# Attention head of a two-layer decoder trunk: the order of ScalarE's and VectorE's work, and which engine copies the transposed probabilities

## The chip, the cores and the metric

One core of one Trainium2 chip runs the whole program. The metric is the time of one execution on the device in microseconds (us). The time before is 2576.37 us, the median of 3 runs (2575.84 to 2578.2).

## The reference, cut to what matters

A trunk of two equal layers over 512 tokens of width 1024, all in float32. Each layer adds a SwiGLU block, a token mixer and a second SwiGLU block to the residual stream. The change lies in the mixer:

```
rq, rk, rv, rg, sq, sk, sv, gate_r, gate_s = split(h @ w_in)
ret = head_groupnorm(retention(rope(rq), rope(rk), rv))       # 4 heads, dk 128, dv 256
ret = silu(rg) * ret
scores = sq_block . k_two_blocks * 64**-0.5, banded mask      # 16 query heads of 64, 2 key heads
m = max(scores, sink);  p = exp(scores - m)
probs = p / (sum(p) + exp(sink - m))
out = probs @ v_two_blocks
merged = sigmoid(gate_r) * (ret @ w_branch_ret) + sigmoid(gate_s) * (out @ w_branch_swa)
x = x + g2 * (merged @ w_out)
```

## The kernel before

**Units.** Every projection is cut into units of 128 output columns (`unit`, L1500). A unit is 8 steps of three products (L1486 to L1488): weights and activations are each split into a high and a low part, and high x high, high x low and low x high are summed in one PSUM bank, `pA[0]` or `pA[1]`, alternately. A unit's weights are loaded by SyncE's queue (`load`, L367) into `raw[s]`, ScalarE writes their high part (`split_weights`, L538), VectorE the low part (`split_weights`, L881), and TensorE starts the unit when the low part is there (`lo_ready`) and the bank is free (`bank_free`). The load of the next weights into the same `raw[s]` waits for that low part too.

**One head of the attention stage.** The stage has 4 turns a layer, 8 in all; here a turn is called a head, the first one head 0. A turn works on one retention head and on four steps of windowed attention, numbered h0 to h0+3, each with 2 query heads and 2 blocks of 128 queries. Between the small products of the attention steps TensorE computes six units: RQ and RK (retention query and key), G0 and G1 (retention gate), and SQ0 and SQ1 (the next turn's attention queries). TensorE's own order isn't changed: scores h0, unit RQ, (`variance` of the turn before), scores h0+1, unit RK, transposes h0, scores h0+2, unit G0, values h0, transposes h0+1, scores h0+3, unit G1, values h0+1, transposes h0+2, retention scores, unit SQ0, values h0+2, transposes h0+3, unit SQ1, values h0+3, retention values and the last retention scores.

**One step.** `swa_scores` (L1588) writes 1024 columns into banks 0 and 1 of `pM`. `maxima` (VectorE, L1150) adds the mask and moves them to `probs[w]` (L1154; its end, `masked`, lets TensorE write the next scores), and takes the row maxima. `exps` (ScalarE, L690) does four exponentials of 256 columns. `normalise` (VectorE, L1168) multiplies by the reciprocal sums. `swa_transposes` (L1597) makes eight 128x128 transposes into banks 2 and 3 of `pM`. `probs_out` copies them to `probs_t`: ScalarE bank 2 (L699 to L701), VectorE bank 3 (L1180 to L1182). `swa_values` (L1604) waits for both copies, and for one bank each:

```
pe.wait_ge(pt_act, no + 1)
pe.wait_ge(pt_dve, no + 1)
```

There is one `probs_t`, and two `probs[w]`, used in turn.

**Other work in the turn.** For the retention query and key ScalarE swaps the halves (`swap`, L680) and VectorE applies the rotation (`rope`, L1135, called by `retention_rope`, L1304). For the gate units ScalarE does Tanh (L799) and VectorE the product (`retention_gate`, L1308). `swa_out` (L703, L1184) splits the attention output of two steps into high and low part. `decay` (L1331) multiplies the retention scores by the decay and releases TensorE's `ret_values` (L1689, L1694). `start_query` swaps and rotates the next turn's queries.

**What sets the order.** Each engine has one queue in an order written out by hand: `middle` (ScalarE L781, VectorE L1300, TensorE L1659), then `tail` (L804, L1328, L1679), in a loop over three turns and once more written out for the last turn, which has no next query and no unit SQ1. An instruction that waits for a semaphore holds up all that is behind it on its engine.

Of the kernel before, what the change touches and what calls it, by code (L numbers as in the profile page):

```python
# [25 lines left out]
RH, DV = 4, 256  # L26
# [83 lines left out]
def decoder(nc, x, c, positions, norm_ffn1, norm_mix, norm_ffn2, final_norm, w_ada, b_ada,  # L110
# [5 lines left out]
    with ctx:  # L116
# [3 lines left out]
        def sem(name):  # L120
            return ctx.enter_context(nc.semaphore(name))
# [104 lines left out]
        swapped, rope_done = sem("swapped"), sem("rope_done")  # L226
        key_in, head_in = sem("key_in"), sem("head_in")
        scores, masked, max_ready, exp_ready, p_ready = sem("scores"), sem("masked"), sem("max_ready"), sem("exp_ready"), sem("p_ready")
        pt_ps, pt_act, pt_dve, o_ps, o_hi, o_done = (sem(n) for n in ("pt_ps", "pt_act", "pt_dve", "o_ps", "o_hi", "o_done"))
        st_ps, st_done, y_ps, ysq, ysum, y_free, var_ps = (sem(n) for n in ("st_ps", "st_done", "y_ps", "ysq", "ysum", "y_free", "var_ps"))  # L230
        mg_ready, mg_hi, mg_lo = sem("mg_ready"), sem("mg_hi"), sem("mg_lo")
        z_ready, y_first, y_last, o_first, o_last, stored = (sem(n) for n in ("z_ready", "y_first", "y_last", "o_first", "o_last", "stored"))
# [300 lines left out]
        def _(act):  # L533
# [163 lines left out]
                last.then_inc(exp_ready, 1)  # L697

            def probs_out(no):  # L699
                act.wait_ge(pt_ps, 2 * no + 1)  # L700
                act.activation(probs_t[:, 0:T], pM[:, 2, :], ACT.Copy).then_inc(pt_act, 1)  # L701

            def swa_out(no, tile):  # L703
                act.wait_ge(o_ps, no + 1)
# [21 lines left out]
            with act.Fori(0, DEPTH) as l:  # L726
# [54 lines left out]
                def middle(i):  # L781
                    b, g = pair_no(l, HEAD0) + 3 * i, gated_no(l, HEAD0) + 3 * i
                    rope0 = LAYER_ROPES * l + 1 + 4 * i
                    h0 = 4 * (RH * l + i)
                    exps(h0, 0)
                    swap(b + 1, 0, g + 1, rope0 + 2, pA[0], P // 2)
                    split_weights(b + 2, 0, UP_UNIT)
                    probs_out(h0)
                    exps(h0 + 1, 1)
                    swap(b + 1, 1, g + 1, rope0 + 3, pA[1], P // 2)  # L790
                    split_weights(b + 2, 1, UP_UNIT)
                    probs_out(h0 + 1)
                    exps(h0 + 2, 0)
                    for s in range(2):
                        act.wait_ge(unit_done, 2 * (b + 2) + s + 3)
                        act.wait_ge(rope_done, rope0 + 4 + 1)
                        if s:
                            act.wait_ge(bank_free[0], g + 2 + 2)
                        act.activation(side, pA[s][:, :], ACT.Tanh, scale=0.5).then_inc(swapped, 1)  # L799
                        split_weights(b + 3, s, UP_UNIT)  # L800
                        if s == 0:
                            exps(h0 + 3, 1)

                def tail(i, start):  # L804
                    h0 = 4 * (RH * l + i)
                    swa_out(2 * (RH * l + i), 2 * i)
                    probs_out(h0 + 2)
                    start(0)
                    probs_out(h0 + 3)
                    start(1)  # L810
                    swa_out(2 * (RH * l + i) + 1, 2 * i + 1)
                    act.wait_ge(y_ps, RH * l + i + 2)
                    for e in range(2):
                        act.activation(probs[1][:, T * e:T * (e + 1)], pM[:, 2 + e, :], ACT.Square).then_inc(ysq, 1)
# [48 lines left out]
        def _(dve):  # L863
# [313 lines left out]
                    last = dve.tensor_scalar(p, p, rden[w][:, n:n + 1], None, ALU.mult)  # L1177
                last.then_inc(p_ready, 1)

            def probs_out(no):  # L1180
                dve.wait_ge(pt_ps, 2 * no + 2)
                dve.tensor_copy(probs_t[:, T:2 * T], pM[:, 3, :]).then_inc(pt_dve, 1)  # L1182

            def swa_out(no, tile):  # L1184
                dve.wait_ge(o_hi, no + 1)
                dve.tensor_tensor(Alo[:, KT + tile, :], pO[:, :], Ahi[:, KT + tile, :].bitcast(F), ALU.subtract).then_inc(o_done, 1)
# [34 lines left out]
            with st.loop(0, DEPTH, LAYER_STEPS) as l:  # L1221
# [78 lines left out]
                def middle(i):  # L1300
                    b, side0, rope0, n0 = numbers(i)
                    h0 = 4 * n0

                    def retention_rope(n, tile):  # L1304
                        rope(rope0 + 2 + n, side0 + 2 + n, pA[n], cos_r, sin_r, [(tile, 0, P)], n)
                        split_weights(b + 2, n, UP_UNIT)

                    def retention_gate(n):  # L1308

                        dve.wait_ge(swapped, side0 + 4 + n + 1)  # L1310
                        dve.scalar_tensor_tensor(silu_g[:, n, :], side, 1.0, pA[n][:, :], ALU.add, ALU.mult).then_inc(bank_free[n], 1)
                        split_weights(b + 3, n, UP_UNIT)

                    retention_rope(0, rq)
                    normalise(h0, 0)
                    maxima(h0 + 1, l, i, 0, 1, 1)
                    probs_out(h0)
                    normalise(h0 + 1, 1)
                    retention_rope(1, rk)
                    maxima(h0 + 2, l, i, 1, 0, 0)  # L1320
                    probs_out(h0 + 1)
                    normalise(h0 + 2, 0)
                    retention_gate(0)
                    maxima(h0 + 3, l, i, 1, 1, 1)
                    retention_gate(1)
                    normalise(h0 + 3, 1)

                def tail(i, next_head):  # L1328
                    b, side0, rope0, n0 = numbers(i)
                    h0 = 4 * n0  # L1330

                    def decay(part):

                        dve.wait_ge(st_ps, RET_PARTS * n0 + part + 1)
                        for n in RET_BLOCKS[part]:
                            w, (bank, at) = T - P * n, RET_AT[n]
                            last = dve.tensor_tensor(ret_s[bank][:, at:at + w], pM[:, bank, at:at + w], K[:, bass.ds(K_DECAY + T * i, w)], ALU.mult)
                        last.then_inc(st_done, 1)

                    swa_out(2 * n0, 2 * i)  # L1340
                    probs_out(h0 + 2)
                    decay(0)
                    decay(1)
                    if next_head:
                        start_query(i + 1, 0)
                        split_weights(b + 4, 0, UP_UNIT)
                    probs_out(h0 + 3)
                    if next_head:
                        start_query(i + 1, 1)
                    swa_out(2 * n0 + 1, 2 * i + 1)  # L1350
                    decay(2)
                    if next_head:
                        split_weights(b + 4, 1, UP_UNIT)
                    for e in range(2):
                        dve.wait_ge(ysq, 2 * n0 + e + 1)
                        dve.tensor_tensor(XV[:, 2 * i + e, :], pM[:, 2 + e, :], silu_g[:, e, :], ALU.mult).then_inc(y_free, 1)
# [70 lines left out]
        def _(pe):  # L1427
# [169 lines left out]
            def swa_transposes(no, w):  # L1597
                pe.wait_ge(p_ready, no + 1)
                for a in range(2):
                    for n in range(4):  # L1600
                        last = pe.transpose(pM[:, 2 + a, P * n:P * (n + 1)], probs[w][:, T * a + P * n:T * a + P * (n + 1)], ident)
                    last.then_inc(pt_ps, 1)

            def swa_values(no, half):  # L1604
                pe.wait_ge(pt_act, no + 1)
                pe.wait_ge(pt_dve, no + 1)
                for n in range(2):
                    blk = 2 * half + n
                    for kt in range(0 if blk else 1, 2):
# [192 lines left out]
```

## Time and profile before

| What | us |
|---|---|
| median of 3 runs | 2576.37 |
| the profiled execution's own time | 2574.76 |
| its span, first to last instruction | 2572.9 |
| attention stage of layer 0 | 508.50 to 732.60 |
| attention stage of layer 1 | 1748 to 1975 |
| one turn in the loop (scores h0 to the next scores h0, 564.47 to 620.53) | 56.06 |

The profile is one execution. Times in its timeline count from the start of the span. A timeline row says start, duration, engine, line, operation, what it writes and reads, and how many instructions are merged in it; a bracket says how long the engine had been idle and which instruction released it. TensorE's products overlap: one of 512 columns lasts 0.39 us, but the next starts 0.23 us after it. TensorE is PE in the rows, VectorE DVE, ScalarE ACT, GpSimd POOL, and PEld is TensorE's loading of weights.

### The profile page before, as it was taken

What the parts mean: (1) busy time and instruction counts of PE and PEld (TensorE: products, weight loads), DVE (VectorE), ACT (ScalarE), POOL (GpSimd) and SP (SyncE); (2) the same over time, 40 slices, a digit from 0 to 9 for tenths busy, and PEclk for the clock granted to TensorE, in tenths of its full rate; (3) what the DMA queues carried; (4) which work ended last, traced back from release to release, by engine and by line L of the source; (5) the groups of instructions that cost most, each with busy time, mean ns of one, the idle gap of its engine ahead of it and who ended that gap; (6) DMA issues with size and microseconds to landing.
All of it is one profiled execution on the core that took longest, in us unless ns stands there. A gap on an engine that the chain in (4) does not pass through costs nothing.

```text
span 2572.9 us, 35974 instructions
## 1 busy us (share of the span) xinstructions
PE 2492.2 (97%) x11573; PEld 2039.4 (79%) x11573; DVE 1535.1 (60%) x2341; ACT 874.2 (34%) x1324; POOL 213.1 (8%) x167
## 2 busy tenths in 40 slices
PE   5999999999999999999999999999999999999998
PEld 4788888877778878888878888887777888788887
DVE  6876778677743367633467767777665445633333
ACT  2321233545423243223332222345543333321232
POOL 5100003000000040000040000120000001200001
PEclk7899999999999999999999999999999999999999
DMA  6465664321223425533326656632111343233332
GB/s 221 123 201 174 182 198 127 123 62 53 57 74 98 128 85 170 158 88 98 103 86 196 186 173 195 180 115 74 57 57 50 98 131 98 82 104 92 90 110 78
DMA packets 494472, 307.19 MB, mean 119 GB/s; under 512 B 8936, under 2 KB 488504, under 8 KB 493752
## 3 DMA queue, kind: packets, MB, share of 16 engines
q1 hardware_dynamic: 426808, 239.10, 31.5%
q10 hardware_dynamic: 67584, 67.12, 8.2%
q8 instruction: 39, 0.64, 0.1%
q14 instruction: 41, 0.34, 0.0%
HBM read 299.89 MB, written 6.29 MB: 119 GB/s over the span
## 4 chain that ended last, share of the span: by engine, by line
PE 77%; DVE 12%; ACT 5%; issue 4%; POOL 1%; DVEq 0%; DMA 0%; ACTq 0%; SPq 0%; POOLq 0%
PE ps_proj L1486 24%; PE ps_proj L1488 24%; PE ps_proj L1487 23%; ACT sb_scratch L695 2%; DVE sb_w_lo L886 2%; DVE sb_small L1157 1%; DVE sb_scratch L1154 1%; PE ps_mid L1642 1%; PE ps_mid L1643 1%; PE ps_mid L1644 1%; DVE sb_scratch L1177 1%; POOL sb_scratch L470 1%; ACT sb_w_hi L542 1%; DVE sb_h_lo L953 1%; DVE sb_scratch L898 1%
## 5 line engine op out<-in xcount | busy, mean ns | idle before, releaser
L1486 PE MATMUL ps_proj<-sb_a_hi,sb_w_hi 128*128 128x512 f32 x1888 | 736.5, 390 | 3.0 <-DVE sb_w_lo L886 3.0
L1488 PE MATMUL ps_proj<-sb_a_hi,sb_w_lo 128*128 128x512 f32 x1888 | 734.8, 389 | 0.0
L1487 PE MATMUL ps_proj<-sb_a_lo,sb_w_hi 128*128 128x512 f32 x1888 | 734.7, 389 | 0.0
L542 ACT ACTIVATE sb_w_hi<-sb_raw 128x1024 fp32r<-128x1024 f32 (+1 forms) x388 | 431.0, 1111 | 872.0 <-PE ps_proj L1488 832.5
L886 DVE TENSOR_TENSOR sb_w_lo<-sb_raw,sb_w_hi 128x1024 fp32r<-128x1024 f32 (+1 forms) x388 | 503.5, 1298 | 310.5 <-ACT sb_w_hi L542 295.1
L1486 PE MATMUL ps_proj<-sb_h_hi,sb_w_hi 128*128 128x512 f32 x1280 | 509.9, 398 | 10.8 <-DVE sb_w_lo L886 6.3
L1487 PE MATMUL ps_proj<-sb_h_lo,sb_w_hi 128*128 128x512 f32 x1280 | 502.4, 392 | 0.0
L1488 PE MATMUL ps_proj<-sb_h_hi,sb_w_lo 128*128 128x512 f32 x1280 | 501.8, 392 | 0.0
L1486 PEld LDWEIGHTS ps_proj<-sb_a_hi,sb_w_hi 128*128 128x128 f32 x1888 | 354.4, 188 | 78.9 <-issue 2.9
L1488 PEld LDWEIGHTS ps_proj<-sb_a_hi,sb_w_lo 128*128 128x128 f32 x1888 | 354.4, 188 | 73.9
L1487 PEld LDWEIGHTS ps_proj<-sb_a_lo,sb_w_hi 128*128 128x128 f32 x1888 | 354.4, 188 | 73.2
L1486 PEld LDWEIGHTS ps_proj<-sb_h_hi,sb_w_hi 128*128 128x128 f32 x1280 | 242.5, 189 | 72.0 <-issue 20.3
L1488 PEld LDWEIGHTS ps_proj<-sb_h_hi,sb_w_lo 128*128 128x128 f32 x1280 | 242.6, 190 | 51.9
L1487 PEld LDWEIGHTS ps_proj<-sb_h_lo,sb_w_hi 128*128 128x128 f32 x1280 | 242.8, 190 | 48.6
L898 DVE SCALAR_TENSOR_TENSOR sb_scratch<-sb_scratch,sb_c_act 128x256 f32<-128x256 f32 x448 | 220.4, 492 | 16.1
L455 POOL TENSOR_TENSOR sb_scratch<-sb_scratch 128x512 f32<-128x512 f32 x42 | 69.0, 1644 | 1755.7 <-ACT sb_scratch L553 1754.9
L1041 DVE SCALAR_TENSOR_TENSOR sb_x_or_values<-ps_proj,sb_half_gate,sb_x_or_values 128x512 f32 (+1 forms) x80 | 60.0, 750 | 204.4 <-PE ps_proj L1488 202.7
L1064 DVE TENSOR_TENSOR sb_scratch<-sb_scratch,ps_proj 128x512 f32<-128x512 f32 x80 | 55.0, 687 | 179.2 <-PE ps_proj L1488 179.2
L640 ACT ACTIVATE sb_scratch<-ps_proj 128x512 f32<-128x512 f32 x80 | 47.9, 599 | 300.5 <-PE ps_proj L1488 300.5
L953 DVE SCALAR_TENSOR_TENSOR sb_h_lo<-sb_x_or_values,sb_gain,sb_h_hi 128x512 fp32r<-128x512 f32 (+1 forms) x48 | 71.2, 1492 | 8.4 <-ACT sb_h_hi L575 7.9
L695 ACT ACTIVATE sb_scratch<-sb_scratch,sb_small 128x256 f32<-128x256 f32 x128 | 63.1, 494 | 0.0
L1067 DVE TENSOR_TENSOR sb_a_lo<-sb_scratch,sb_a_hi 128x512 f32 (+1 forms) x80 | 54.7, 684 | 0.0
(171 smaller groups left out, 1804.9 us busy)
## 6 DMA issues: line engine op xcount, KB each, us to landing
sb_raw<-in_ffn_w_up SPq DMA_DIRECT2D x176, 512.0 KB, 3.8
sb_scratch<-in_w_ada ACTq DMA_DIRECT2D x128, 512.0 KB, 4.2
sb_raw<-in_w_in SPq DMA_DIRECT2D x100, 512.0 KB, 3.8
sb_raw<-in_ffn_w_down SPq DMA_DIRECT2D x64, 704.0 KB, 4.5
sb_raw<-in_w_branch_swa SPq DMA_DIRECT2D x16, 512.0 KB, 3.5
sb_raw<-in_w_branch_ret SPq DMA_DIRECT2D x16, 512.0 KB, 3.6
sb_raw<-in_w_out SPq DMA_DIRECT2D x16, 512.0 KB, 3.5
sb_scratch<-in_w_ada SPq DMA_DIRECT2D x14, 512.0 KB, 7.9
```

The costliest lines, as they stand in the source:

```text
L455: pool.tensor_tensor(square_sum, square_sum, squares[:, k % 2, :], ALU.add).then_inc(sq_used, 1)
L542: act.activation(Whi[s][:, 0:n], raw[s][:, 0:n], ACT.Copy).then_inc(hi_ready, 1)
L695: last = act.activation(p, p, ACT.Exp, bias=neg_m[w][:, n:n + 1], scale=HD ** -0.5, accum_out=row_sum[w][:, n:n + 1])
L886: dve.tensor_tensor(Wlo[s][:, 0:n], raw[s][:, 0:n], Whi[s][:, 0:n].bitcast(F), ALU.subtract).then_inc(lo_ready, 1)
L898: ins = dve.scalar_tensor_tensor(ada_acc, ada_raw[s][:, k % 4, :], col, ada_acc, ALU.mult, ALU.add)
L953: dve.scalar_tensor_tensor(Hlo[:, k, :], XV[:, k, :], gain[:, bass.ds(k, 1)], Hhi[:, k, :].bitcast(F), ALU.mult, ALU.subtract).then_inc(gx ...
L1041: dve.scalar_tensor_tensor(XV[:, m, :], pA[s][:, :], half_gate[:, bass.ds(m, 1)], XV[:, m, :], ALU.mult, ALU.add).then_inc(bank_free[s], 1)
L1064: dve.tensor_tensor(work, side, pA[1][:, :], ALU.mult).then_inc(bank_free[1], 1)
L1067: dve.tensor_tensor(Alo[:, i, :], work, Ahi[:, i, :].bitcast(F), ALU.subtract).then_inc(act_lo, 1)
L1486: pe.matmul(bank, Whi[s][:, w], hi, start=first, stop=False)
L1487: pe.matmul(bank, Whi[s][:, w], lo, start=False, stop=False)
L1488: return pe.matmul(bank, Wlo[s][:, w], hi, start=False, stop=last)
```

## The change

The copy of the transposed probabilities is one ScalarE instruction of 1024 columns. It is released once all eight transposes are done, where before each bank had a release of its own. VectorE's copy and the semaphore `pt_dve` are gone. On ScalarE the swap of unit RK comes ahead of the copy of step h0; the Tanh of G0 ahead of the copy of step h0+1; the Tanh of G1, `swa_out` and the copy of step h0+2 ahead of the exponentials of step h0+3. On VectorE `normalise` of h0 comes ahead of the first rotation, the second rotation ahead of `normalise` of h0+1, the product of G0 ahead of `normalise` of h0+2; the low part of G0's weights stays behind the first rotation, those of G1, SQ0 and SQ1 come behind `normalise` of h0+1, h0+2 and h0+3; `swa_out` comes ahead of the product of G1, and the first two parts of `decay` ahead of `normalise` of h0+3.

```diff
 # ScalarE
             def probs_out(no):
-                act.wait_ge(pt_ps, 2 * no + 1)
-                act.activation(probs_t[:, 0:T], pM[:, 2, :], ACT.Copy).then_inc(pt_act, 1)
+                act.wait_ge(pt_ps, no + 1)
+                act.activation(probs_t.rearrange("p (a t) -> p a t", a=2), pM[:, 2:4, :], ACT.Copy).then_inc(pt_act, 1)
...
                     exps(h0, 0)
                     swap(b + 1, 0, g + 1, rope0 + 2, pA[0], P // 2)
                     split_weights(b + 2, 0, UP_UNIT)
+                    swap(b + 1, 1, g + 1, rope0 + 3, pA[1], P // 2)
                     probs_out(h0)
                     exps(h0 + 1, 1)
-                    swap(b + 1, 1, g + 1, rope0 + 3, pA[1], P // 2)
                     split_weights(b + 2, 1, UP_UNIT)
-                    probs_out(h0 + 1)
-                    exps(h0 + 2, 0)
-                    for s in range(2):
+
+                    def gate(s):
                         act.wait_ge(unit_done, 2 * (b + 2) + s + 3)
                         act.wait_ge(rope_done, rope0 + 4 + 1)
                         if s:
                             act.wait_ge(bank_free[0], g + 2 + 2)
                         act.activation(side, pA[s][:, :], ACT.Tanh, scale=0.5).then_inc(swapped, 1)
-                        split_weights(b + 3, s, UP_UNIT)
-                        if s == 0:
-                            exps(h0 + 3, 1)
+
+                    gate(0)
+                    probs_out(h0 + 1)
+                    exps(h0 + 2, 0)
+                    split_weights(b + 3, 0, UP_UNIT)
+                    gate(1)
+                    swa_out(2 * (RH * l + i), 2 * i)
+                    probs_out(h0 + 2)
+                    exps(h0 + 3, 1)
+                    split_weights(b + 3, 1, UP_UNIT)
 
                 def tail(i, start):
                     h0 = 4 * (RH * l + i)
-                    swa_out(2 * (RH * l + i), 2 * i)
-                    probs_out(h0 + 2)
                     start(0)
                     probs_out(h0 + 3)
                     start(1)
 # VectorE
-            def probs_out(no):
-                dve.wait_ge(pt_ps, 2 * no + 2)
-                dve.tensor_copy(probs_t[:, T:2 * T], pM[:, 3, :]).then_inc(pt_dve, 1)
...
                     def retention_rope(n, tile):
                         rope(rope0 + 2 + n, side0 + 2 + n, pA[n], cos_r, sin_r, [(tile, 0, P)], n)
-                        split_weights(b + 2, n, UP_UNIT)
...
                         dve.scalar_tensor_tensor(silu_g[:, n, :], side, 1.0, pA[n][:, :], ALU.add, ALU.mult).then_inc(bank_free[n], 1)
-                        split_weights(b + 3, n, UP_UNIT)
...
+                    normalise(h0, 0)
                     retention_rope(0, rq)
-                    normalise(h0, 0)
+                    split_weights(b + 2, 0, UP_UNIT)
                     maxima(h0 + 1, l, i, 0, 1, 1)
-                    probs_out(h0)
+                    retention_rope(1, rk)
                     normalise(h0 + 1, 1)
-                    retention_rope(1, rk)
+                    split_weights(b + 2, 1, UP_UNIT)
                     maxima(h0 + 2, l, i, 1, 0, 0)
-                    probs_out(h0 + 1)
+                    retention_gate(0)
                     normalise(h0 + 2, 0)
-                    retention_gate(0)
+                    split_weights(b + 3, 0, UP_UNIT)
                     maxima(h0 + 3, l, i, 1, 1, 1)
+                    swa_out(2 * n0, 2 * i)
                     retention_gate(1)
+                    decay(i, 0)
+                    decay(i, 1)
                     normalise(h0 + 3, 1)
+                    split_weights(b + 3, 1, UP_UNIT)
...
                 def tail(i, next_head):
...
-                    swa_out(2 * n0, 2 * i)
-                    probs_out(h0 + 2)
-                    decay(0)
-                    decay(1)
                     if next_head:
                         start_query(i + 1, 0)
                         split_weights(b + 4, 0, UP_UNIT)
-                    probs_out(h0 + 3)
                     if next_head:
                         start_query(i + 1, 1)
                     swa_out(2 * n0 + 1, 2 * i + 1)
-                    decay(2)
+                    decay(i, 2)
 # TensorE
                 for a in range(2):
                     for n in range(4):
                         last = pe.transpose(pM[:, 2 + a, P * n:P * (n + 1)], probs[w][:, T * a + P * n:T * a + P * (n + 1)], ident)
-                    last.then_inc(pt_ps, 1)
+                last.then_inc(pt_ps, 1)
...
                 pe.wait_ge(pt_act, no + 1)
-                pe.wait_ge(pt_dve, no + 1)
```

## Rows read from the trace of the kernel before

**Rows 1.** The page, part 1: busy time of each engine over the span.

```profile
PE 2492.2 (97%) x11573; PEld 2039.4 (79%) x11573; DVE 1535.1 (60%) x2341; ACT 874.2 (34%) x1324; POOL 213.1 (8%) x167
```

**Rows 2.** Busy time by window, layer 0's attention stage: stretch, length, engines, clock, DMA.

```profile
508.50:732.60 224.10, 212.59 (x1178) 162.80 (x1177) 155.13 (x286) 111.04 (x256) 10.06 (x11) 1.00 0.20 57
```

**Rows 3.** TensorE's waits, 508 to 735 us: total us, times, longest.

```profile
PE ps_o L1612 <- DVE sb_scratch L1182: 7.5, 5, 1.7
PE ps_mid L1593 <- DVE sb_scratch L1154: 2.3, 4, 1.1
PE ps_mid L1694 <- DVE sb_scratch L1337: 1.7, 3, 0.6
```

**Rows 4.** Timeline of TensorE, head 1 of layer 0.

```profile
578.63 1.03 PE L1601 MATMUL ps_mid<-sb_consts,sb_scratch 128*128 128x128 f32 x8
579.59 1.14 PE L1593 MATMUL ps_mid<-sb_scratch 64*128 64x256 f32 x8
...
586.04 0.39 PE L1488 MATMUL ps_proj<-sb_h_hi,sb_w_lo 128*128 128x512 f32 x1
586.36 0.88 PE L1612 MATMUL ps_o<-sb_scratch 128*64 128x128 f32 x12
587.17 1.09 PE L1601 MATMUL ps_mid<-sb_consts,sb_scratch 128*128 128x128 f32 x8
588.68 1.14 PE L1593 MATMUL ps_mid<-sb_scratch 64*128 64x256 f32 x8 [0.42 <-DVE sb_scratch L1154]
...
597.37 1.89 PE L1686 MATMUL ps_mid<-sb_scratch 128*128 128x512 f32 x6
...
604.36 0.39 PE L1488 MATMUL ps_proj<-sb_h_hi,sb_w_lo 128*128 128x512 f32 x1
606.42 0.88 PE L1612 MATMUL ps_o<-sb_scratch 128*64 128x128 f32 x12 [1.67 <-DVE sb_scratch L1182]
...
619.47 1.13 PE L1694 MATMUL ps_mid<-sb_scratch 128*128 128x256 f32 x4 [0.57 <-DVE sb_scratch L1337]
```

**Rows 5.** Timeline of TensorE in head 0 and in head 3, the last.

```profile
532.62 1.14 PE L1593 MATMUL ps_mid<-sb_scratch 64*128 64x256 f32 x8 [1.10 <-DVE sb_scratch L1154]
...
719.26 1.09 PE L1601 MATMUL ps_mid<-sb_consts,sb_scratch 128*128 128x128 f32 x8
721.23 1.09 PE L1612 MATMUL ps_o<-sb_scratch 128*64 128x128 f32 x16 [0.88 <-DVE sb_scratch L1182]
```

**Rows 6.** Timeline of VectorE, head 1.

```profile
582.88 0.16 DVE L1171 TENSOR_TENSOR sb_small<-sb_small 128x4 f32<-128x4 f32 x1 [1.59 <-ACT sb_scratch L695]
...
584.35 0.69 DVE L1139 TENSOR_TENSOR sb_scratch<-ps_proj,sb_cos_r 128x512 f32<-128x512 f32 x1
...
586.28 1.22 DVE L886 TENSOR_TENSOR sb_w_lo<-sb_raw,sb_w_hi 128x1024 fp32r<-128x1024 f32 x1
587.41 1.22 DVE L1154 TENSOR_TENSOR sb_scratch<-ps_mid,sb_consts 128x1024 f32<-128x1024 f32 x1
...
590.36 0.69 DVE L1182 COPY sb_scratch<-ps_mid 128x512 f32<-128x512 f32 x1
...
605.59 0.68 DVE L1182 COPY sb_scratch<-ps_mid 128x512 f32<-128x512 f32 x1
```

**Rows 7.** Timeline of ScalarE, head 1.

```profile
580.67 0.21 ACT L692 ACTIVATE sb_small<-sb_small 128x4 f32<-128x4 f32 x1 [0.81 <-DVE sb_small L1166]
...
582.87 0.60 ACT L686 ACTIVATE sb_scratch<-ps_proj 64x512 f32<-64x512 f32 x1
...
584.10 1.06 ACT L542 ACTIVATE sb_w_hi<-sb_raw 128x1024 fp32r<-128x1024 f32 x1
...
592.52 0.58 ACT L799 ACTIVATE sb_scratch<-ps_proj 128x512 f32<-128x512 f32 x1
...
602.73 0.58 ACT L701 ACTIVATE sb_scratch<-ps_mid 128x512 f32<-128x512 f32 x1
```

**Rows 8.** The page, part 6: SyncE's loads of the mixer's weights, us to landing.

```profile
sb_raw<-in_w_in SPq DMA_DIRECT2D x100, 512.0 KB, 3.8
```

More of the change, by code:

```diff
@@ L228, in decoder @@
         scores, masked, max_ready, exp_ready, p_ready = sem("scores"), sem("masked"), sem("max_ready"), sem("exp_ready"), sem("p_ready")
-        pt_ps, pt_act, pt_dve, o_ps, o_hi, o_done = (sem(n) for n in ("pt_ps", "pt_act", "pt_dve", "o_ps", "o_hi", "o_done"))
+        pt_ps, pt_act, o_ps, o_hi, o_done = (sem(n) for n in ("pt_ps", "pt_act", "o_ps", "o_hi", "o_done"))
         st_ps, st_done, y_ps, ysq, ysum, y_free, var_ps = (sem(n) for n in ("st_ps", "st_done", "y_ps", "ysq", "ysum", "y_free", "var_ps"))
@@ L1311, in retention_gate, with decay @@
                         dve.scalar_tensor_tensor(silu_g[:, n, :], side, 1.0, pA[n][:, :], ALU.add, ALU.mult).then_inc(bank_free[n], 1)
-                        split_weights(b + 3, n, UP_UNIT)
+                    normalise(h0, 0)
                     retention_rope(0, rq)
-                    normalise(h0, 0)
+                    split_weights(b + 2, 0, UP_UNIT)
                     maxima(h0 + 1, l, i, 0, 1, 1)
-                    probs_out(h0)
+                    retention_rope(1, rk)
                     normalise(h0 + 1, 1)
-                    retention_rope(1, rk)
+                    split_weights(b + 2, 1, UP_UNIT)
                     maxima(h0 + 2, l, i, 1, 0, 0)
-                    probs_out(h0 + 1)
+                    retention_gate(0)
                     normalise(h0 + 2, 0)
-                    retention_gate(0)
+                    split_weights(b + 3, 0, UP_UNIT)
                     maxima(h0 + 3, l, i, 1, 1, 1)
+                    swa_out(2 * n0, 2 * i)
                     retention_gate(1)
+                    decay(i, 0)
+                    decay(i, 1)
                     normalise(h0 + 3, 1)
+                    split_weights(b + 3, 1, UP_UNIT)
+                def decay(i, part):
+                    dve.wait_ge(st_ps, RET_PARTS * numbers(i)[3] + part + 1)
+                    for n in RET_BLOCKS[part]:
+                        w, (bank, at) = T - P * n, RET_AT[n]
+                        last = dve.tensor_tensor(ret_s[bank][:, at:at + w], pM[:, bank, at:at + w], K[:, bass.ds(K_DECAY + T * i, w)], ALU.mult)
+                    last.then_inc(st_done, 1)
                 def tail(i, next_head):
@@ L1330, in tail @@
                     h0 = 4 * n0
[L1332 to L1338, printed above, removed]
-                    swa_out(2 * n0, 2 * i)
-                    probs_out(h0 + 2)
-                    decay(0)
-                    decay(1)
                     if next_head:
```

## The prediction

> **What bounds the kernel now.** I read the page's busy times first [rows 1]: TensorE is busy for 97% of the span, VectorE for 60%, ScalarE for 34%. A change in the order of ScalarE and VectorE can therefore only win what TensorE waits. The busy time by window [rows 2] shows how much that is where the change lies: in layer 0's attention stage TensorE works 212.59 of 224.10 us, so some 11.5 us are open there, at a granted clock of 1.00 (the 2.4 GHz level), which these short waits haven't lowered. VectorE works 155 us of the stage and ScalarE 111, so neither is full. The list of waits [rows 3] names the 11.5 us: 7.5 us of the value products (L1612) for VectorE's copy L1182, 2.3 us of the scores (L1593) for VectorE's masking L1154, and 1.7 us of the last retention values (L1694) for the decay L1337. Layer 1's stage has the same three lines with the same totals.
>
> TensorE's timeline of head 1 [rows 4] shows where in the turn. Scores h0+3 start at 588.68 after 0.42 us idle. Values h0+2, behind unit SQ0, start at 606.42 after 1.67 us idle. The last retention values wait 0.57 us at 619.47. Head 0 has 1.10 us at the first place, and head 3 has an additional wait of 0.88 us at values h0+3, which there stand right behind their transposes [rows 5].
>
> The waits cost a little more than the idle figures, which start from modelled ends. Between transposes and scores nothing waits at 578.63 and 579.59, 0.96 us apart; at 587.17 and 588.68 they are 1.51 apart, so that wait costs 0.55. From a unit's last product to values it is 0.32 us without a wait (586.04 to 586.36) and 2.06 with it (604.36 to 606.42): 1.74 [rows 4].
>
> **The change part by part, walked through head 1.** Up to the transposes at 578.63 nothing moves. `normalise` of h0 fits into VectorE's idle time ahead of the first rotation, and the low part of G0's weights and the maxima of h0+1 end no later than before.
>
> *Scores h0+3.* They need the masking of h0+2. Before, VectorE did `normalise`, the rotation of RK, the low part of G1 and only then the masking, from 587.41 to 588.63 [rows 6]; the rotation lay in the chain behind the exponentials. Now it lies beside them. The new chain: unit RK ends at about 578.8, ScalarE begins its swap at 579.0, which takes 1.23 (582.87 to 584.10) [rows 7], to 580.2. Then the copy of 1024 columns. The trace has no such copy from PSUM. Its lower bound is ScalarE's 1024 columns from SBUF, 1.06; its upper bound two copies of 512 at 0.58 to 0.60, so 1.20 [rows 7]. I take 1.06, the nearest in shape: 581.3. Exponentials 2.20 (580.67 to 582.87): 583.5. `normalise` 1.47 (582.88 to 584.35): 585.0. Low part of G1 1.13 (586.28 to 587.41): 586.1. Masking 1.22: 587.3 [rows 6]. The rotation of RK, 1.93 (584.35 to 586.28), runs from 580.2 to 582.1 while ScalarE does copy and exponentials. TensorE could start the scores at 587.17 + 0.96 = 588.13. So the wait goes, with 0.8 us to spare, 0.6 with the dearer copy. Head 0 stands the same way to its chain: its 1.10 us goes too.
>
> *Retention scores.* These need the masking of h0+3. The chain begins at G0's end, 586.4. Tanh to 587.2; copy of h0+1 behind the transposes' end (587.17 + 1.09) to 589.4, by when the maxima of h0+2 are there as well (586.1 + 2.95, the 2.95 from 587.41 to 590.36 [rows 6]); exponentials to 591.6; `normalise` to 593.0; low part of SQ0 to 594.2; masking to 595.4. TensorE is there at 597.37 - 0.55 = 596.8 [rows 4]: 1.4 us to spare. What waits behind ScalarE's Tanh here is exactly this copy and these exponentials, so this is the chain that could go wrong.
>
> *Values h0+2.* Before, VectorE's copy stood behind the product of G1, a low part, `normalise` and `swa_out`, and began at 605.59 [rows 6], although ScalarE's half had begun at 602.73 [rows 7]. Now ScalarE's copy follows the transposes at 597.0 and ends at 598.1, and VectorE's `swa_out` ends at 597.8. TensorE is there at 604.36 + 0.32 - 0.55 = 604.1. The 1.74 us goes, with 6 to spare. What is late next: `normalise` of h0+3 (exponentials 598.1 to 600.3, the two decays by then done, 601.8) against the transposes at 604.9, and the low part of SQ1 at 602.9 against its unit at 605.9; 3 us each. Later waits up to the end of the turn have 2.5 us or more by the same working.
>
> *Last retention values.* Swap, rotation, `swa_out` and decay stand in the same order behind unit SQ1, so the 0.57 us stays.
>
> *Values h0+3 in head 3.* Here nothing covers the copy: the transposes end at 720.35, and the values start 0.88 later, at 721.23 [rows 5], with VectorE's copy of 0.69 [rows 6] in between. Now it is 1.06 (to 1.20) on ScalarE: 0.4 us more, 0.5 at most.
>
> *What costs nothing, and what hides it.* VectorE loses 32 copies of 0.69, 22 us; it is not the bound. ScalarE goes from 32 x 0.59 to 32 x 1.06, 15 us more, hidden by units of 24 products, 5.5 us each; without them each copy would cost the 0.4 of head 3. SyncE's loads wait for the low parts, which come at 586.1, 594.2 and 602.9 against 587.4, 595.9 and 603.5; they are issued sooner, and a load lands in 3.8 us [rows 8], long before its split. No DMA is issued from the moved steps, GpSimd's waits hang on TensorE alone. One wait fewer before 32 groups of values is worth nothing, or at best 0.1 us a group, 3 us in all, since values show a gap of 0.32 where products show 0.23; I take nothing and keep the 3 us for the lower end.
>
> **Sum.** Of the idle figures of a layer 2.3 + (7.5 - 0.88) = 8.9 go [rows 3, 5]. The four waits of either kind cost 0.13 and 0.07 more than shown: + 0.8. The last copy: - 0.4. That is 9.3 a layer, 18.7 in both with roundings. The profiled execution's own time is 2574.76 (span 2572.9), which gives 2556.1; it lies 1.6 below the median of the runs, which gives 2557.7, my forecast, 0.73% less.
>
> **A rule that speaks against it.** The values of a step are released when the later copy ends. Half the copy takes VectorE 0.69, and ScalarE 0.58 beside it, and one engine needs 1.06 at least for the whole [rows 6, 7]. The Trainium skill, "PSUM — Partial Sum Buffer", Specifications (TRN2), says that ScalarE and VectorE can read PSUM in parallel at full bandwidth if they don't meet in a bank; by that rule the split copy is the better one, and taking it away costs time. The trace agrees only where TensorE has nothing in between.
>
> **The rivals.**
> *The copy lies on the path everywhere.* Each of the 32 groups of values would start some 0.37 us later instead of 2: 30 x 0.37 = 11 us back, 2568.8. The parallel reading of two banks, above, is the reason one could give. Against it: in three of four steps a unit of 5.5 us lies between transposes and values.
> *The scores' wait stays.* The chain to the masking of h0+2 has only 0.8 us to spare, and now holds swap, copy and exponentials in one ScalarE queue. If the chain is 1.4 us longer than I have it, the 2.3 + 4 x 0.13 = 2.8 us a layer remain: 5.6 more, 2563.3.
> *ScalarE's queue becomes the bound, slower than before.* Place: Tanh of G0 ahead of the copy of h0+1 and the exponentials of h0+2, and through `normalise`, low part and masking the retention scores. It decides from 1.4 us on. To end 5 us above the time before it has to give back 18.7 + 5, or 3.0 us in each of 8 heads, so the chain must be 4.4 us longer than I have it. Priced at 4.6, TensorE waits 3.2 us a head, 25.6 in all: 2583. For it: the chain is serial over two engines. Against it: Tanh stood directly behind exponentials before too and took 0.58 us [rows 7], with no reload of the activation table before it.
> That the change doesn't do what it says can hardly be: the orders are written out by hand.
>
> **How the numbers follow.** The forecast has 0.80, the scores' wait that stays (wholly or in part) 0.10, the copy on the path 0.04, slower 0.03, other small losses that leave the time within 5 us of before 0.03. A measurement of this kernel can tell about 0.2%, 5 us, from no change. Faster: 0.94; within 0.2%: 0.03; slower: 0.03. The range reaches down by the 3 us for the fewer waits, with 0.7 for the runs' spread, to 2554.0, and up to the second rival, 2563.5.
>
> **What would show it.** TensorE's waits should name L1154 and the copy nowhere but in head 3, there with 1.2 to 1.3 us; L1694 keeps 3 waits of 0.57 a layer. A turn takes 53.8 us instead of 56.06. ScalarE's copy takes 1.06 to 1.20 us, 32 times. VectorE's L1154 of step h0+2 ends some 0.8 us before its scores. Scores still waiting for L1154 would be the second rival; a new line with L1177, L1154 before L1686, or an additional table load, the third. The prediction is wrong if the turn isn't between 53.3 and 54.6 us.

## The result, and the profile after

The kernel after takes 2557.01 us, the median of 4 runs (2555.9 to 2558.24), against 2576.11 us for the kernel before (4 runs, 2574.15 to 2578.2). The ratio is 0.9926, with a 95% interval of 0.9909 to 0.9943: faster by 0.74%. The forecast was 2557.7, with a range of 2554.0 to 2563.5. The profiled execution of after took 2558.24 us, its span is 2556.5.

The page, part 1, of the kernel after answers to [rows 1]:

```profile
PE 2493.7 (98%) x11573; PEld 2041.7 (80%) x11573; DVE 1515.6 (59%) x2309; ACT 887.8 (35%) x1324; POOL 212.8 (8%) x167
```

TensorE does the same 11573 products in nearly the same busy time (1.5 us more), but in a span that is 16.4 us shorter. VectorE has 32 instructions and 19.5 us less busy time, ScalarE as many instructions as before and 13.6 us more.

Busy time by window of layer 0's attention stage in the kernel after, the answer to [rows 2]:

```profile
508.20:723.20 215.00, 212.16 (x1178) 162.69 (x1178) 145.62 (x270) 117.86 (x256) 9.93 (x11) 1.00 0.21 59
```

The stage is 9.1 us shorter (224.10 to 215.00), TensorE's work in it is the same: 212.6 and 212.2 us. Some 2.8 us of it are open where it was 11.5.

TensorE's waits in that stage of the kernel after (total us, times, longest), the answer to [rows 3]:

```profile
PE ps_mid L1691 <- DVE sb_scratch L1336: 1.7, 3, 0.6
PE ps_o L1609 <- ACT sb_scratch L701: 1.1, 1, 1.1
```

The scores' wait for the masking is gone, and of the 7.5 us of the value products one wait of 1.1 us is left, the last turn's. The wait for the decay is as it was. Layer 1 has the same two lines with the same totals.

TensorE's timeline in head 1 of the kernel after, the answer to [rows 4]; its turn begins 3.2 us sooner than before:

```profile
575.45 1.03 PE L1599 MATMUL ps_mid<-sb_consts,sb_scratch 128*128 128x128 f32 x8
576.41 1.14 PE L1591 MATMUL ps_mid<-sb_scratch 64*128 64x256 f32 x8
...
583.99 1.09 PE L1599 MATMUL ps_mid<-sb_consts,sb_scratch 128*128 128x128 f32 x8
585.01 1.13 PE L1591 MATMUL ps_mid<-sb_scratch 64*128 64x256 f32 x8
...
593.74 1.89 PE L1683 MATMUL ps_mid<-sb_scratch 128*128 128x512 f32 x6
...
600.73 0.39 PE L1486 MATMUL ps_proj<-sb_h_hi,sb_w_lo 128*128 128x512 f32 x1
601.05 0.88 PE L1609 MATMUL ps_o<-sb_scratch 128*64 128x128 f32 x12
...
614.10 1.13 PE L1691 MATMUL ps_mid<-sb_scratch 128*128 128x256 f32 x4 [0.57 <-DVE sb_scratch L1336]
615.16 1.14 PE L1591 MATMUL ps_mid<-sb_scratch 64*128 64x256 f32 x8
```

Between the second transposes and the scores there are 1.02 us, between the last product of SQ0 and the values 0.32, and neither row has a bracket. The previous turn's scores h0 stand at 561.28, so a turn takes 53.88 us, against 56.06.

VectorE's timeline of the same head, and below it ScalarE's, the answers to [rows 6] and [rows 7]:

```profile
577.10 0.69 DVE L1143 TENSOR_TENSOR sb_scratch<-ps_proj,sb_cos_r 128x512 f32<-128x512 f32 x1 [1.03 <-ACT sb_scratch L687]
...
580.11 0.16 DVE L1175 TENSOR_TENSOR sb_small<-sb_small 128x4 f32<-128x4 f32 x1 [1.00 <-ACT sb_scratch L695]
...
581.58 1.22 DVE L890 TENSOR_TENSOR sb_w_lo<-sb_raw,sb_w_hi 128x1024 fp32r<-128x1024 f32 x1
582.72 1.22 DVE L1158 TENSOR_TENSOR sb_scratch<-ps_mid,sb_consts 128x1024 f32<-128x1024 f32 x1
...
590.84 1.22 DVE L1158 TENSOR_TENSOR sb_scratch<-ps_mid,sb_consts 128x1024 f32<-128x1024 f32 x1
...
593.83 0.69 DVE L1186 TENSOR_TENSOR sb_a_lo<-ps_o,sb_a_hi 128x512 f32 x1
```

```profile
575.78 0.59 ACT L686 ACTIVATE sb_scratch<-ps_proj 64x512 f32<-64x512 f32 x1 [4.95 <-PE ps_proj L1486]
...
577.00 1.02 ACT L701 ACTIVATE sb_scratch<-ps_mid 128x1024 f32<-128x1024 f32 x1
577.92 0.20 ACT L692 ACTIVATE sb_small<-sb_small 128x4 f32<-128x4 f32 x1
...
583.37 0.60 ACT L798 ACTIVATE sb_scratch<-ps_proj 128x512 f32<-128x512 f32 x1 [2.34 <-PE ps_proj L1486]
...
593.94 1.02 ACT L701 ACTIVATE sb_scratch<-ps_mid 128x1024 f32<-128x1024 f32 x1 [0.29 <-PE ps_mid L1599]
```

The rotation of unit RK (577.10) now runs while ScalarE copies (577.00) and takes the exponentials (577.92); `normalise` follows at 580.11. The masking of h0+2 (582.72) ends at 583.94, and scores h0+3, which wait for it, start at 585.01: 1.0 us to spare.

The last turn of the kernel after, the answer to [rows 5]: the last transposes, ScalarE's copy, and the values that wait for it.

```profile
709.60 1.09 PE L1599 MATMUL ps_mid<-sb_consts,sb_scratch 128*128 128x128 f32 x8
710.73 1.02 ACT L701 ACTIVATE sb_scratch<-ps_mid 128x1024 f32<-128x1024 f32 x1 [5.01 <-PE ps_mid L1599]
711.81 1.09 PE L1609 MATMUL ps_o<-sb_scratch 128*64 128x128 f32 x16 [1.11 <-ACT sb_scratch L701]
```

### The profile page after: what moved, and what is told of

Its sections match the earlier page's. It is cut to its first block, busy times and chain, and to the rows that moved or that the text cites. A ratio compares the mean times of both kernels' runs of the same rounds, so it can differ in the third digit from the quotient of the medians.

```text
span 2556.5 us, 35860 instructions
## 1 busy us (share of the span) xinstructions
PE 2493.7 (98%) x11573; PEld 2041.7 (80%) x11573; DVE 1515.6 (59%) x2309; ACT 887.8 (35%) x1324; POOL 212.8 (8%) x167
## 4 chain that ended last, share of the span: by engine, by line
PE 90%; DVE 5%; issue 2%; ACT 1%; POOL 1%; DMA 0%; DVEq 0%; SPq 0%; ACTq 0%; POOLq 0%
PE ps_proj L1484 27%; PE ps_proj L1486 27%; PE ps_proj L1485 27%; PE ps_mid L1591 1%; PE ps_mid L1599 1%; PE ps_mid L1639 1%; PE ps_mid L1641 1%; PE ps_mid L1640 1%; PE ps_o L1609 1%; POOL sb_scratch L470 1%; DVE sb_h_lo L957 1%; DVE sb_scratch L902 1%; PE ps_mid L1691 1%; PE ps_mid L1683 1%; DVE sb_scratch L1202 0%
## 5 line engine op out<-in xcount | busy, mean ns | idle before, releaser
L686 ACT ACTIVATE sb_scratch<-ps_proj 32x512 f32<-32x512 f32 (+1 forms) x48 | 28.3, 590 | 81.6 <-PE ps_proj L1486 81.3
```

## The experiments

Theory: the gain comes from two serial chains over ScalarE and VectorE, which the new order shortens; the copy's engine matters little. First rival: it comes from who copies. The runs were made in two groups, each on one chip beside the kernel before: e1, e2, e3 and e8 beside 12 runs of it with a median of 2576.13 us, e4 to e7 beside 15 runs with 2575.19. "Above after" and "below after" compare a median with the 2557.01 us of the section above, so with e4 to e7 they can be off by the 0.9 us between the groups. Times in head 1 are of layer 0.

Medians of this kernel move by a microsecond or two. The traces tell small differences better: the time from a layer's first scores to its last row of retention values agrees between the two layers within 0.1 us. Here it is for both layers together.

| Kernel | both stages, us | against before | against after |
|---|---|---|---|
| before | 431.9 | | |
| after | 413.8 | -18.1 | |
| e1_copy_alone | 426.9 | -5.0 | |
| e2_order_alone | 413.4 | -18.5 | -0.4 |
| e3_first_half_old | 417.1 | | +3.3 |
| e8_second_half_old | 416.0 | | +2.2 |
| e4_one_spare | 413.8 | | 0.0 |
| e5_four_spare | 425.7 | | +12.0 |
| e6_decay_first | 410.2 | | -3.6 |
| e7_both | 409.5 | | -4.3 |

**The copy alone, on the old order** (e1_copy_alone)

```diff
 # on the kernel before
-                act.wait_ge(pt_ps, 2 * no + 1)
-                act.activation(probs_t[:, 0:T], pM[:, 2, :], ACT.Copy).then_inc(pt_act, 1)
+                act.wait_ge(pt_ps, no + 1)
+                act.activation(probs_t.rearrange("p (a t) -> p a t", a=2), pM[:, 2:4, :], ACT.Copy).then_inc(pt_act, 1)
 # and VectorE's probs_out with its four calls, and pt_dve, are gone
```

> The kernel before, with the copy of all 1024 columns on ScalarE and none on VectorE, both orders as before. Theory (the gain comes from the order of the two queues): values h0+2 no longer wait for VectorE's copy, but the low part of swa_out right ahead of it on VectorE ended at 605.67, so they start some 0.65 us sooner a head and keep about 1.0 us of idle time; the wait at scores h0+3 stays (0.42 to 0.5), values h0+3 of the last head wait 0.4 longer. Together 8 x 0.65 - 2 x 0.4 = 4.4 us less than before, about 2571.7. Rival (the gain comes from who copies, that is from VectorE's 22 us): all of it is here, 2557 to 2559.

Measured: 2569.88 us (8 runs), ratio 0.9975 (0.9964 to 0.9985), 6.3 us below the 2576.13 of before. TensorE's waits in layer 0's attention stage:

```profile
PE ps_o L1603 <- DVE sb_a_lo L1182: 3.8, 4, 1.0
PE ps_mid L1585 <- DVE sb_scratch L1154: 2.3, 4, 1.1
PE ps_mid L1685 <- DVE sb_scratch L1331: 1.7, 3, 0.6
PE ps_o L1603 <- ACT sb_scratch L701: 1.1, 1, 1.1
```

Expected were 4.4 us less, and the stages became 5.0 shorter. So the copy's removal alone gives about a third of the gain, as its interval has it 4 to 9 us. The values then wait for the low part of `swa_out`, which had stood directly ahead of VectorE's copy: 0.95 us four times in place of 1.65. The scores' 2.3 us is untouched.

**The order alone, with the split copy** (e2_order_alone)

```diff
 # on the kernel after; both copies, releases and waits as in the kernel before, and VectorE's copies here:
+                    probs_out(h0)
                     retention_rope(1, rk)
...
                     retention_gate(0)
+                    probs_out(h0 + 1)
                     normalise(h0 + 2, 0)
...
                     decay(i, 1)
+                    probs_out(h0 + 2)
                     normalise(h0 + 3, 1)
...
                         split_weights(b + 4, 0, UP_UNIT)
+                    probs_out(h0 + 3)
```

> The kernel after, with the split copy put back (ScalarE bank 2, VectorE bank 3, a release for each bank), VectorE's copies ahead of the second rotation, ahead of normalise of h0+2, of normalise of h0+3, and behind the first next query. Theory: VectorE's 0.69 us fits into its idle time each time, so TensorE's waits are those of after, and the last head's is 0.4 us shorter: 0.7 to 0.9 us below after, about 2556.3, a turn of 53.9. Rival (who copies): most of the gain is lost, 2570 or more. The PSUM rule as a price everywhere would give 11 us below after, 2546.

Measured: 2557.82 us (5 runs, 2554.59 to 2558.93), ratio 0.9926 (0.9912 to 0.9939). TensorE's waits:

```profile
PE ps_mid L1700 <- DVE sb_scratch L1343: 1.7, 3, 0.6
PE ps_o L1618 <- DVE sb_scratch L1186: 0.9, 1, 0.9
```

The order alone gives the whole gain, as far as the runs can tell. The two parts don't add: the 6.3 us of the copy's removal are contained in the 18.3 of the order, since the copy only cost something where the order had it stand late. The last turn's wait is 0.9 instead of 1.1 us; the 0.4 us in two layers that this is worth show in the stages' time and can't be seen in the medians. The first rival falls.

**The first half of the turn in the old order** (e3_first_half_old)

```diff
 # on the kernel after
-                    swap(b + 1, 1, g + 1, rope0 + 3, pA[1], P // 2)
                     probs_out(h0)
                     exps(h0 + 1, 1)
+                    swap(b + 1, 1, g + 1, rope0 + 3, pA[1], P // 2)
...
-                    retention_rope(1, rk)
                     normalise(h0 + 1, 1)
+                    retention_rope(1, rk)
```

> The kernel after, with only the swap and the rotation of unit RK put back behind the exponentials and normalise of h0+1. Theory: the masking of h0+2 ends at about 585.4 in head 1 instead of 583.9, so scores h0+3 wait about 0.4 us again (1.1 in head 0), 5 to 6 us in all: 2562.5; values h0+2 don't wait. Rival (the second half of the turn is the only one that counts, the first has slack): no wait at the scores, 2557.

Measured: 2560.16 us (5 runs, 2559.76 to 2563.17), ratio 0.9939 (0.9926 to 0.9953), 3.2 us above after. In TensorE's waits one line has come back:

```profile
PE ps_mid L1591 <- DVE sb_scratch L1158: 1.4, 4, 0.4
```

So the rotation in the chain is what made the scores wait. From the transposes' start to the masking's end it is 9.94 us in head 1 (576.62 to 586.56), where after has 8.49 (575.45 to 583.94). The rotation adds 1.93, and the swap, which no longer stands ahead of the copy, gives some 0.5 back; of the 1.45 us, 1.1 were to spare, and 0.35 is the wait.

The wait is 0.35 us in head 0 too, where the kernel before had 1.10 and the theory expected 1.1 again. The start of head 0's exponentials of h0+1 shows the difference, first in the kernel before, then in this run:

```profile
524.58 0.20 ACT L692 ACTIVATE sb_small<-sb_small 128x4 f32<-128x4 f32 x1 [1.43 <-DVE sb_small L1166]
```

```profile
524.32 0.20 ACT L692 ACTIVATE sb_small<-sb_small 128x4 f32<-128x4 f32 x1
```

Before, ScalarE stood idle for 1.43 us, waiting for the maxima of h0+1, which VectorE took only behind `normalise` of h0 (1.46 us, 520.11 to 521.57). In e3 that `normalise` still stands ahead of the first rotation, and the exponentials follow the copy without a pause, 15.36 us from the head's first scores where it was 16.03: 0.67 of the 0.75 us between the two waits. So a second piece of the new order helps head 0. This is read from the rows; no run undid that piece alone.

**The second half in the old order** (e8_second_half_old)

```diff
 # on the kernel after, ScalarE
-                    gate(0)
                     probs_out(h0 + 1)
                     exps(h0 + 2, 0)
+                    gate(0)
                     split_weights(b + 3, 0, UP_UNIT)
+                    exps(h0 + 3, 1)
                     gate(1)
+                    split_weights(b + 3, 1, UP_UNIT)
                     swa_out(2 * (RH * l + i), 2 * i)
                     probs_out(h0 + 2)
-                    exps(h0 + 3, 1)
-                    split_weights(b + 3, 1, UP_UNIT)
 # VectorE
-                    retention_gate(0)
                     normalise(h0 + 2, 0)
+                    retention_gate(0)
                     split_weights(b + 3, 0, UP_UNIT)
                     maxima(h0 + 3, l, i, 1, 1, 1)
+                    retention_gate(1)
+                    split_weights(b + 3, 1, UP_UNIT)
+                    normalise(h0 + 3, 1)
                     swa_out(2 * n0, 2 * i)
-                    retention_gate(1)
                     decay(i, 0)
                     decay(i, 1)
-                    normalise(h0 + 3, 1)
-                    split_weights(b + 3, 1, UP_UNIT)
```

> The kernel after, with the second half of the turn (from the copy of h0+1 on) in the order of before on ScalarE and VectorE, but with the copy on ScalarE alone. Theory: scores h0+3 don't wait; VectorE's low part of swa_out comes behind the product of G1, a low part and normalise of h0+3 and ends at about 601.5 of head 1, where TensorE wants the values at 601.05: 0.4 to 0.5 us a head, 3.5 to 4 us in all, 2561. Rival (both halves are needed in full, as the wait at values h0+2 was 1.67): the wait is back at 1.2 or more a head, 2567 or more.

Measured: 2560.42 us (5 runs, 2558.97 to 2562.53), ratio 0.9938 (0.9924 to 0.9951), 3.4 us above after. In TensorE's waits the values wait again, for `swa_out`:

```profile
PE ps_o L1609 <- DVE sb_a_lo L1186: 0.8, 4, 0.2
```

The wait is 0.2 us a head, where 0.4 to 0.5 was expected, and nothing like the 1.67 of before. Its four waits a layer and what starts cost above the idle time explain the 2.2 us by which the stages are longer; the rest of the 3.4 is within the spread of the runs. With e3 and e8 over 80% of the gain stays (16.0 and 15.7 us below before, of 19.1): with the one copy and the other half of the new order each chain misses its time by little.

**How much the first chain has to spare** (e4_one_spare, e5_four_spare)

```diff
 # on the kernel after, ScalarE; 1 copy in the first run, 4 in the second, each behind the one before it
                     probs_out(h0)
+                    for n in range(4):
+                        if n:
+                            act.wait_ge(spared, 4 * (RH * l + i) + n)
+                        act.activation(spare[:, :], cos_r[:, :], ACT.Copy).then_inc(spared, 1)
                     exps(h0 + 1, 1)
```

> The kernel after, with one spare ScalarE copy of 512 columns into an unused tile between the copy of h0 and the exponentials of h0+1 (0.5 to 0.65 us more in that chain, 8 times). Theory: in the profile of after the masking of h0+2 ends at 583.94 and its scores start at 585.01, so the chain has some 1.0 us to spare: no wait at scores h0+3, time as after, 2557. Rival (the chain is at its limit, and every microsecond in ScalarE's queue costs): + 8 x 0.55 = 4.4 us, 2561.

> The same with four spare copies one behind the other, 2.4 to 2.6 us more in the chain. Theory: TensorE waits 1.4 to 1.6 us at scores h0+3 in each of 8 heads, 12 us in all, 2569; the later waits stay away, because what is late at the scores is late for TensorE too. Rival (slack of more than 2.5 us, as the later chains have): time as after.

Measured: 2558.19 us with one spare copy (4 runs, 2557.45 to 2559.25; ratio 0.9933, 0.9917 to 0.9948). This median, 1.2 us above after, lies between theory and rival and doesn't decide; the trace does, with the waits of after and stages as long as its own. With four it is 2570.09 us (10 runs, 2567.45 to 2571.81; ratio 0.9979, 0.997 to 0.9989), 13.1 above after, and the stages are 12.0 longer, where 12 was expected. ScalarE's timeline with four, then TensorE's waits:

```profile
579.98 2.62 ACT L795 ACTIVATE sb_spare<-sb_cos_r 128x512 f32<-128x512 f32 x4
582.51 0.19 ACT L694 ACTIVATE sb_small<-sb_small 128x4 f32<-128x4 f32 x1
```

```profile
PE ps_mid L1597 <- DVE sb_scratch L1164: 4.7, 4, 1.2
...
PE ps_mid L1605 <- DVE sb_scratch L1187: 0.8, 4, 0.2
```

The chain is 2.5 us longer (579.98 to 582.51), and 1.4 us a head appear as idle time, in two places: 1.17 at the scores, and 0.19 already at the transposes of h0+1, which wait for `normalise`. With the 1.0 us to spare the sum closes. The theory had missed the transposes: in after `normalise` of h0+1 ends 2.3 us ahead of them (581.67 against 583.99), less than the 2.5 us added.

**The wait that was left** (e6_decay_first)

```diff
 # on the kernel after, VectorE's tail
-                    swa_out(2 * n0 + 1, 2 * i + 1)
                     decay(i, 2)
+                    swa_out(2 * n0 + 1, 2 * i + 1)
```

> The kernel after, with the last part of decay ahead of the second swa_out on VectorE. Theory: in after decay starts at 613.63 behind a rotation that ends at 613.1 and swa_out of 0.6, while its scores are there at 611.8; it now starts at 613.03, ends 0.6 sooner, and the wait of 0.57 at the last retention values goes, three times a layer: 3.4 us, 2553.6. Rival (the wait moves to ScalarE's squares and the next maxima): the idle time at L1691 goes and the turn stays at 53.9.

Measured: 2553.78 us (5 runs, 2552.94 to 2557.75), ratio 0.9918 (0.9905 to 0.9932), 3.2 us below after by the medians (2.3 by the ratios to before) and 3.6 by the stages' time, where 3.4 was expected. One wait is left in the stage, and the turn, from 561.28 to the row below, takes 53.28 us:

```profile
PE ps_o L1609 <- ACT sb_scratch L701: 1.1, 1, 1.1
```

```profile
614.56 1.14 PE L1591 MATMUL ps_mid<-sb_scratch 64*128 64x256 f32 x8
```

So nothing behind the retention values took the wait's place.

**The split copy where nothing covers it** (e7_both)

```diff
 # on e6_decay_first, for the last turn's last step alone
+            def half_probs_out(no):       # ScalarE
+                act.wait_ge(pt_ps, no + 1)
+                act.activation(probs_t[:, 0:T], pM[:, 2, :], ACT.Copy).then_inc(pt_act, 1)
+            def half_probs_out(no):       # VectorE
+                dve.wait_ge(pt_ps, no + 1)
+                dve.tensor_copy(probs_t[:, T:2 * T], pM[:, 3, :]).then_inc(pt_dve, 1)
...
+                    if isinstance(i, int):
+                        pe.wait_ge(pt_dve, l + 1)
                     swa_values(h0 + 3, 1).then_inc(o_ps, 1)
```

> As e6, and in the last turn of a layer alone the last step's copy is split again, ScalarE bank 2 and VectorE bank 3, both released after all eight transposes. Theory: there the wait falls from 1.11 to about 0.8 (copies of 0.69 and 0.60 beside each other instead of 1.02), 0.6 us in both layers below e6, about 2553.0; a 4.0 us win on after.

Measured: 2554.52 us (5 runs, 2551.83 to 2555.92), ratio 0.9914 (0.9901 to 0.9928), 0.7 above e6 where 0.6 below it was expected. ScalarE's and VectorE's copies in the last turn, and TensorE's wait in the stage:

```profile
710.13 0.60 ACT L705 ACTIVATE sb_scratch<-ps_mid 128x512 f32<-128x512 f32 x1 [5.01 <-PE ps_mid L1609]
710.13 0.69 DVE L1190 COPY sb_scratch<-ps_mid 128x512 f32<-128x512 f32 x1 [3.25 <-PE ps_mid L1609]
```

```profile
PE ps_o L1619 <- DVE sb_scratch L1190: 0.8, 1, 0.8
```

The two copies start together and last as long as alone, and the wait falls by 0.3 us, as expected. The stages are 0.7 us shorter than in e6, which is below what the medians can tell; as the runs don't separate the two, the simpler e6 is the version to keep.

## Why the prediction was right

**Scores h0+3.** The forecast had the chain from RK's end to the masking's end at 8.5 us (578.8 to 587.3) with 0.8 to spare; the trace of after has 8.3 us and 1.0 to spare. The copy of 1024 columns, which the trace of before did not show, took 1.02 us (bounds 1.06 to 1.20, value taken 1.06, so it fell a little below the lower bound). The wait is gone in all heads, and e3 shows that it was the rotation's place; in head 0 the earlier `normalise` of h0 has a part in it, which the forecast had not worked out.

**Retention scores.** The masking of h0+3 was to end at 595.4 against scores due at 596.8. After, it takes VectorE 1.22 us from 590.84 and ends at 592.06, and the retention scores start at 593.74 without a wait: 1.7 us to spare, where 1.4 was forecast. No run lengthened this chain.

**Values h0+2.** The 1.74 us a head went; ScalarE's copy ends at 594.96 (593.94 + 1.02) and the values start at 601.05, so the forecast 6 us to spare are 6.1.

**Last retention values.** Predicted to stay at 0.57, and it is there at 614.10. e6 shows that it hung on the order of two VectorE instructions.

**Values h0+3 in the last turn.** Predicted 1.2 to 1.3 us, measured 1.11, so the difference to before is 0.23, not 0.4. The forecast took the copies' difference, 1.06 - 0.69. Measured it is 1.02 - 0.69 = 0.33, and the values start 0.06 us behind the copy's end (711.75 to 711.81), where it was 0.15 before:

```profile
720.39 0.69 DVE L1182 COPY sb_scratch<-ps_mid 128x512 f32<-128x512 f32 x1 [0.83 <-PE ps_mid L1601]
```

This copy ends at 721.08, and the values start at 721.23. Why they follow sooner now was not tried.

**One wait fewer before the values** was taken as nothing. The gap from the last product to the values is 0.32 us as before (600.73 to 601.05), so where the copy is long done it is nothing.

**The sum.** Predicted 9.3 us a layer; in both layers the stage became 9.1 shorter, 18.1 in all against 18.7. The idle figures went as forecast. What the waits cost beyond them was taken as 0.8 us a layer and comes to 0.4: at scores h0+3 the forecast took 0.96 us between transposes and scores without a wait, and in after it is 1.02, so that wait had cost 0.49 and not 0.55. The last copy's 0.23 in place of 0.4 makes up a part of it. The medians differ by 19.1, with an interval of 14.7 to 23.4, so that 18.7 and 19.1 lie so close together is in part luck. The two profiled executions differ by only 16.4 us in span; what the clock has to do with that is told below.

**What the prediction read wrongly, without harm.** A unit lies between transposes and values not in three of four steps but in all four of a turn, but for the last turn's last step: in 15 of 16 a layer. That speaks against the copy on the path more strongly than the prediction had it. Its list of waits leaves out the transposes of h0+1, which wait for `normalise` and had 2.3 us to spare, less than the later waits. And VectorE's 22 us are a sum of durations; its busy time, in which neighbouring instructions overlap, fell by 19.5.

**The rivals.** The copy on the path everywhere: no; values wait for the copy only in the last turn, and e2 with the split copy is not faster. In e7 the halves take 0.60 and 0.69 us beside each other, as long as alone in the kernel before, and that brings 0.3 us a layer. The Trainium skill's rule, that ScalarE and VectorE can read PSUM in parallel at full bandwidth if they don't meet in a bank ("PSUM — Partial Sum Buffer", Specifications (TRN2)), is borne out by this. The scores' wait that stays: the chain needed 1.0 us more to bring it back, and e4 and e5 stand on the two sides of that. ScalarE's queue as the bound: TensorE's L1683 doesn't wait for VectorE's L1158, there is no additional table load (9 in both kernels), and a turn takes 53.88 us.

## What to carry to other kernels

When an engine of 60% load holds up one of 97%, follow the serial chain from the event that starts it to the wait that ends last, and take out of it what could run beside it: here a rotation of 1.93 us moved into the time in which the other engine did its exponentials. Where work of TensorE covers it, a copy's cost is where it stands in a queue, not how long it lasts: to take 19.5 us off VectorE's busy time was worth 5 to 6 us in the old order and nothing that could be measured in the new one. Only in the last turn, where nothing covers it, does its length count. Before you move work to another engine, write down the slack of every wait behind it; of the waits that went away, the scores' has the least, 1.0 us, and four spare copies showed what comes beyond it, in part at transposes that the list had left out.

## What the runs showed of the hardware that was not expected

In both kernels the granted clock of TensorE falls for some microseconds at the start of each SwiGLU block but the first, where TensorE has worked with hardly a pause and then waits some 3 us for the reciprocal root (3.4, 2.7 and 3.4 us in the kernel before). At the same place of the mixer it waits 1.0 us, and the clock stays at 1.00. How far the mean falls differs between executions. Three stretches of 30 us from 10 us ahead of that place, in busy time by window (the clock is the third value from the end): the kernel before, then the kernel after.

```profile
945.00:975.00 30.00, 26.59 (x127) 22.28 (x126) 25.27 (x37) 12.51 (x18) 14.45 (x12) 0.94 0.20 56
1315.00:1345.00 30.00, 27.31 (x131) 23.14 (x130) 24.46 (x37) 10.07 (x15) 9.59 (x8) 0.94 0.28 88
2192.00:2222.00 30.00, 26.59 (x127) 22.50 (x126) 24.65 (x37) 12.51 (x17) 14.25 (x12) 0.94 0.20 59
```

```profile
936.00:966.00 30.00, 26.59 (x123) 22.43 (x121) 24.05 (x36) 11.60 (x16) 14.01 (x12) 0.89 0.18 53
1307.00:1337.00 30.00, 27.11 (x130) 22.99 (x130) 24.64 (x38) 10.42 (x14) 9.09 (x8) 0.94 0.31 92
2174.00:2204.00 30.00, 26.59 (x123) 22.43 (x122) 23.32 (x36) 11.81 (x16) 14.75 (x12) 0.89 0.19 55
```

In the kernel before products start 0.43 us apart from 955.96 on, the lower of the two levels (1.2 GHz), and 0.23 apart again from 959.69 on. The wait in the first and third stretch is 3.4 us in both kernels, and the time that TensorE is busy is equal too, 26.59 us, but after does 4 products fewer in it, at 0.89 instead of 0.94: at 0.23 us each 0.9 us a stretch. That fits what lies outside the attention stages. From the last retention values of layer 0 to the first scores of layer 1 the kernel after takes 1.0 us more than before, and from layer 1's to the end of the span 1.1 more, each with one of the stretches at 0.89 in it; with 0.3 less ahead of the first stage that leaves 16.4 of the stages' 18.1 us.

The fall is not even certain. In e3_first_half_old the first stretch (938 to 968) has the same wait of 3.4 us and a clock of 1.00, and the second has 1.00 in e1, e4 and e5. Between e6_decay_first (0.94 three times, span 2551.6) and e7_both (0.94, 0.89, 0.89, span 2554.1) it hides the 0.7 us that e7's stages are shorter. What decides it was not tried. It means that one profiled execution of this kernel can be off by 2 to 3 us, through stages that a change doesn't touch, and that the stage's own time is the better measure of such a change.
